# q, k and v computed row tile by row tile while the first modulation arrives by columns

## The reference

```
mod = c @ w_ada + b_ada                       # (1, 6*1024), c is (1, 1024)
sh1, sc1, gt1, sh2, sc2, gt2 = split(mod, 6)
h = rms_norm(x, g_pre_mix) * (1 + sc1) + sh1
proj = h @ w_in                               # 1024 x 5120
bg, cg, u, q, k, v, ga, gb = split(proj, [512]*6 + [1024]*2)
y_conv = short_conv(bg, cg, u) @ w_proj_conv
y_attn = stick_breaking_attention(q, k, v) @ w_proj_attn   # 8 heads of 64
merged = sigmoid(ga) * y_conv + sigmoid(gb) * y_attn
x = x + gt1 * rms_norm(merged @ w_out, g_post_mix)
...                                           # MLP with sh2, sc2, gt2; then layer two
```

## Time and profile before

| | |
|---|---|
| median of 3 runs | 845.17 us (841.72 to 845.89) |
| the profiled execution | 843.94 us, of which the span is 841.9 us |
| PE busy | 791.7 us, 94% of the span |
| DVE busy | 524.4 us, 62% |
| ACT busy | 379.3 us, 45% |
| POOL busy | 136.3 us, 16% |
| mean granted clock of PE | 0.946 |

### The profile page before, as it was taken

One profiled execution on the slowest core, in us unless ns is written; L12 is line 12 of the kernel. 1 busy time (PEld: TensorE's weight loads), 2 busy tenths in 40 slices (PEclk: granted clock), 3 DMA queues, 4 the chain that ended last, 5 costly groups with the idle time before them and its releaser, 6 DMA issues.

```text
span 841.9 us, 14038 instructions
## 1 busy us (share of the span) xinstructions
PE 791.7 (94%) x6051; PEld 754.8 (90%) x6051; DVE 524.4 (62%) x675; ACT 379.3 (45%) x520; POOL 136.3 (16%) x129
## 2 busy tenths in 40 slices
PE   3599999999979999999998999899799999999997
PEld 3599889999979999999997998587599999999997
DVE  5886677677336776644436799967654665555441
ACT  3443333443523545543434446577653543443441
POOL 1500110001000000000001399804000122221000
PEclk9599999999959999999997989999899999999998
DMA  9979565776603886565551441141614465654511
GB/s 350 359 261 307 183 201 191 238 272 200 200 1 106 254 277 209 191 210 166 191 157 51 150 152 50 50 151 51 199 51 151 151 220 181 200 175 151 188 39 51
DMA packets 123825, 146.00 MB, mean 173 GB/s; under 512 B 3988, under 2 KB 114804, under 8 KB 123764
## 3 DMA queue, kind: packets, MB, share of 16 engines
q1 hardware_dynamic: 122400, 143.32, 51.8%
q10 hardware_dynamic: 1364, 1.79, 0.7%
HBM read 144.05 MB, written 1.05 MB: 172 GB/s over the span
## 4 chain that ended last, share of the span: by engine, by line
PE 82%; DVE 10%; issue 4%; ACT 2%; DMA 1%; POOL 0%; SPq 0%; ACTq 0%; DVEq 0%; POOLq 0%
PE bank L575 70%; DVE mod_acc L1410 2%; PE bank L621 2%; PE bank L602 2%; ACT w_hi L1028 1%; DMA raw<-in_w_ada 1%; DVE score L1772 1%; DVE w_lo L1418 1%; DVE neg_max L1777 1%; DVE wide L1711 1%; PE bank L812 1%; DVE score L1795 1%; PE bank L798 1%; PE bank L610 1%; PE bank L783 1%
## 5 line engine op out<-in xcount | busy, mean ns | idle before, releaser
L1418 DVE TENSOR_TENSOR w_lo<-raw,w_hi 128x2048 fp32r<-128x2048 f32 (+1 forms) x108 | 245.9, 2280 | 140.6 <-ACT w_hi L1028 140.4
L1028 ACT ACTIVATE w_hi<-raw 128x2048 fp32r<-128x2048 f32 (+1 forms) x110 | 206.5, 1882 | 246.7 <-PE bank L575 227.5
L575 PE MATMUL bank<-act_hi,w_hi 128*128 128x256 f32 x816 | 237.2, 291 | 5.5 <-ACT act_hi L1184 2.7
L575 PE MATMUL bank<-act_lo,w_hi 128*128 128x256 f32 x816 | 234.8, 288 | 0.8 <-DVE act_lo L1678 0.4
L575 PE MATMUL bank<-act_hi,w_lo 128*128 128x256 f32 x816 | 234.1, 287 | 0.7 <-DVE w_lo L1418 0.7
L575 PEld LDWEIGHTS bank<-act_hi,w_hi 128*128 128x128 f32 x816 | 160.1, 196 | 9.1 <-issue 8.1
L575 PEld LDWEIGHTS bank<-act_lo,w_hi 128*128 128x128 f32 x816 | 160.0, 196 | 1.9 <-DVE act_lo L1678 0.7
L575 PEld LDWEIGHTS bank<-act_hi,w_lo 128*128 128x128 f32 x816 | 160.0, 196 | 0.9 <-DVE w_lo L1418 0.9
L575 PE MATMUL bank<-hidden_hi,w_hi 128*128 128x256 f32 x432 | 122.5, 284 | 0.8 <-DVE wide L1976 0.8
L575 PE MATMUL bank<-hidden_hi,w_lo 128*128 128x256 f32 x432 | 122.2, 283 | 0.0
L575 PE MATMUL bank<-hidden_lo,w_hi 128*128 128x256 f32 x432 | 122.2, 283 | 0.0
(11 more groups left out here) (268 smaller groups left out, 1052.3 us busy)
## 6 DMA issues: line engine op xcount, KB each, us to landing
raw<-in_w_in SPq DMA_DIRECT2D x31, 1024.0 KB, 5.8
raw<-in_w_ada SPq DMA_DIRECT2D x24, 1024.0 KB, 6.8
raw<-in_w_gate_up SPq DMA_DIRECT2D x22, 1024.0 KB, 5.1
raw<-in_w_mlp_in SPq DMA_DIRECT2D x16, 1024.0 KB, 5.7
raw<-in_w_mlp_out SPq DMA_DIRECT2D x16, 1024.0 KB, 5.2
raw<-in_w_out SPq DMA_DIRECT2D x8, 1024.0 KB, 7.1
raw<-in_w_down SPq DMA_DIRECT2D x8, 1024.0 KB, 5.1
raw<-in_w_down SPq DMA_DIRECT2D x4, 768.0 KB, 4.4
```

Source lines behind the costliest of these rows:

```text
L575: i = e.matmul(dst, lhs, rhs, start=start and k == 0 and m == 0 and n == 0, stop=stop and k == kt - 1 and n == 2, skip_group_check=True)
L1028: e.activation(w_hi[slot][:, 0:kt * n_cols], raw[i % N_RAW][:, 0:kt * n_cols], ACT.Copy).then_inc(hi_split, 1)
L1418: e.tensor_tensor(w_lo[slot][:, 0:kt * n_cols], raw[i % N_RAW][:, 0:kt * n_cols], w_hi[slot][:, 0:kt * n_cols].bitcast(F32), ALU.subtract) ...
```

## The change

The eight chunks of w_ada for shift and scale are replaced by eight transfers `ada1`, each of 128 columns of the shift and the same 128 of the scale over all 1024 rows (two transfers of 0.5 MB with pieces of 512 bytes). The six products of q, k and v are replaced by eight row-tile products: a chunk is one row tile (128 rows) by all 1536 columns (768 KB with pieces of 6 KB), and gives 36 matmuls (6 banks, 2 halves, 3 passes) that accumulate in six banks at once. The two kinds alternate in `plan`. For row tile k:

- DVE forms six of the eight terms of c times w_ada for both vectors at once (`first_rows`, 128x256 each), PE adds the other two straight from `raw` and sums over partitions (`first_modulation`, 6 matmuls of one column), DVE writes shift and scale of this tile (two operations on one column).
- DVE multiplies x_T by rstd (this was POOL's work), ACT applies scale and shift twice, once into act_hi and once in place, DVE subtracts for act_lo.
- The sums over partitions for tile k+1 stand in PE's program after half of the matmuls of tile k.

The sum of squares of x is taken by ACT over the rows as they landed, and spread to all partitions by two matmuls; the small row loads of the ACT queue go to SP's behind the first four chunks. q, k and v are evacuated by six copies on DVE after the last row tile, and `low` of the first chunk of c stands behind these copies in DVE's program. The remaining 14 products go through four banks, and 12 chunks of w_ada stand among the 18 products from c0 to the projections, two after every three. (Some semaphores are merged with others and their counts renumbered.)

```diff
-        ada_order = [(v, r) for v in (SCALE1, SHIFT1, GATE1, SHIFT2, SCALE2, GATE2) for r in range(ADA_CHUNKS)]
-        IN1, PC = 0, 20
+        ada_order = [(v, r) for v in (GATE1, SHIFT2, SCALE2, GATE2) for r in range(ADA_CHUNKS)]
+        IN1 = DT
+        PC = IN1 + len(in1_order)
...
-            if n % 2 and (n < 6 * ADA_CHUNKS or MLP1 + 2 <= n < MLP1 + 2 + 2 * ADA_CHUNKS):
+            if IN1 <= n < OUT1 and (n - IN1) % 3 != 2 or MLP1 + 2 <= n < MLP1 + 2 + 2 * ADA_CHUNKS and n % 2:
                 plan_ada()
-        for _ in range(2 * ADA_CHUNKS):
-            plan_ada()
+        def plan_first_ada(k):
+            plan.append(("ada1", k, [w("w_ada")[:, v * D + k * P:v * D + (k + 1) * P] for v in (SHIFT1, SCALE1)]))
+        for k in range(DT):
+            plan_first_ada(k)
+            plan_product(first_in1[k * P:(k + 1) * P, :])
...
+        FIRST_BANKS = {("q", 0): 4, ("q", 1): 5, ("k", 0): 6, ("k", 1): 0, ("v", 0): 1, ("v", 1): 2}
+        MOD1_BANKS = (7, 3)
...
-            for i in range(DT // 2):
-                sum_tiles((2 * i, 2 * i + 1), i == 0, i == DT // 2 - 1, (squared, i + 1))
-            modulation_sum(SCALE1)
-            transpose_rows(1)
-            transpose_rows(2)
-            modulation_sum(SHIFT1)
+            pe.wait_ge(x_rstd, 1)
+            for tt in range(TT):
+                t = e.matmul(b[:, tt * P:(tt + 1) * P], x_col[:, 1, tt:tt + 1].to_broadcast([P, P]), ident[:],
+                             start=tt == 0, stop=tt == TT - 1, skip_group_check=True)
+            t.then_inc(x_spread, 1)
+            def first_modulation(k):
...
+                pe.wait_ge(*landed(i))
+                for v in range(2):
+                    for r in range(DVE_ROWS, DT):
+                        e.matmul(b[:, v:v + 1], src[:, v, r, :], cols("c", r, 1), start=v == 0 and r == DVE_ROWS, stop=False,
+                                 skip_group_check=True)
+                pe.wait_ge(ada1_scaled, DVE_ROWS * (k + 1))
+                for v in range(2):
+                    t = e.matmul(b[:, v:v + 1], ada1_acc[:, k % 2, v, :], ones[:, 0:1], start=False, stop=True,
+                                 skip_group_check=True)
+                t.then_inc(mod1_summed, 1)
+            first_modulation(0)
+            for k in range(DT):
+                for c, (name, i) in enumerate(FIRST_BANKS):
+                    if c == 3 and k < DT - 1:
+                        first_modulation(k + 1)
...
+                    for m in range(2):
+                        for n, (wp, ap) in enumerate(((w_hi[slot], act_hi), (w_hi[slot], act_lo), (w_lo[slot], act_hi))):
...
+                t.then_inc(product_done, 1)
...
+            for k in range(DT):
+                high(k)
+                act.wait_ge(y_normed, k + 1)
+                act.wait_ge(mod1_set, 2 * k + 2)
+                e.activation(act_hi[:, k, :], y, ACT.Identity, scale=scale1[:, k:k + 1],
+                             bias=shift1[:, k:k + 1]).then_inc(tiles_hi, 1)
+                e.activation(y, y, ACT.Identity, scale=scale1[:, k:k + 1], bias=shift1[:, k:k + 1]).then_inc(tile_made, 1)
...
             for k in range(DT):
-                dve.wait_ge(tiles_hi, k + 1)
-                e.scalar_tensor_tensor(out=act_lo[:, k, :], in0=wide[1][:, k, :],
...
+                first_rows(k)
+                if k == 0:
+                    dve.wait_ge(x_rms, 1)
+                    e.reciprocal(x_col[:, 1, :], x_col[:, 0, :]).then_inc(x_rstd, 1)
+                first_norm(k)
+                first_modulation(k)
+                low(k)
+                dve.wait_ge(tile_made, k + 1)
+                e.tensor_tensor(act_lo[:, k, :], wide[1][:, k, :], act_hi[:, k, :].bitcast(F32),
+                                ALU.subtract).then_inc(tiles_lo, 1)
...
+            for name in ("q", "k", "v"):
+                for i in range(2):
+                    src = pair(bank[FIRST_BANKS[name, i]])
+                    dve.wait_ge(product_done, IN1)
...
+            stream_to(product_at[IN1])
+            low_after(product_at[IN1 - 2])
```

More of the change, by code:

```diff
@@ L347, in raw_view, with landed @@
             source = plan[i][2]
+            if plan[i][0] == "ada1":
+                return raw[i % N_RAW][:, 0:2 * DT * P].rearrange("p (v r c) -> p v r c", r=DT, v=2)
             kt, n_cols = source.shape[0] // P, source.shape[1]
             return raw[i % N_RAW][:, 0:kt * n_cols].rearrange("p (k c) -> p k c", k=kt)
+        def landed(i):
+            slot = i % N_RAW
+            return raw_landed[slot], sum(32 if plan[j][0] == "ada1" else 16 for j in range(slot, i + 1, N_RAW))
         rows_landed = [sem(f"rows{i}_landed") for i in range(3)]
@@ L521, in build, with ada1_at @@
         S_BANKS, T_BANK, O_BANK = (4, 5), 6, 7
-        mod_no = {v: n for n, v in enumerate((SCALE1, SHIFT1, GATE1, SHIFT2, SCALE2, GATE2))}
+        mod_no = {v: n for n, v in enumerate((GATE1, SHIFT2, SCALE2, GATE2))}
+        def ada1_at(k):
+            return plan.index(next(x for x in plan if x[0] == "ada1" and x[1] == k))
         def sync_program(e):
@@ L681, in stick_output @@
                          stop=True, skip_group_check=True).then_inc(stick_out, 1)
-            for p, (name, i) in enumerate(in1_order):
-                step = p - 6
-                if 0 <= step < HEADS:
+            for step in range(len(in1_order)):
+                p = IN1 + step
+                if step < HEADS:
                     stick_scores(step)
@@ L823, in compress @@
                     pe.wait_ge(cmp_paired_act, KV if not second else 2 * KV)
-                    pe.wait_ge(rms_set, 3 if second else 2)
-                pe.wait_ge(raw_landed[i % N_RAW], 16 * (i // N_RAW + 1))
+                    pe.wait_ge(rms_set, 2 if second else 1)
+                pe.wait_ge(*landed(i))
                 src = raw_view(i)
@@ L1060, in scalar_program @@
-            root(0, D, 1)
-            act.wait_ge(gains_set, 2)
-            act.wait_ge(x_copied, DT // 2)
+                e.activation(x_T[:, 2 * i:2 * i + 2, :], pair(bank[banks.bank["x", i]]), ACT.Copy).then_inc(x_copied, 1)
+            act.wait_ge(x_spread, 1)
+            e.activation(rstd[:], bank[banks.bank["x_rstd"]][:, 0:T], ACT.Copy).then_inc(rstd_set, 1)
             for k in range(DT):
-                e.activation(wide[1][:, k, :], x_T[:, k, :], ACT.Copy, scale=scale1[:, k:k + 1]).then_inc(y_scaled, 1)
@@ new lines, in first_rows @@
+            def first_rows(k):
+                i = ada1_at(k)
+                acc, src = ada1_acc[:, k % 2], raw_view(i)
+                dve.wait_ge(*landed(i))
+                if k >= 2:
+                    dve.wait_ge(mod1_summed, k - 1)
+                for r in range(DVE_ROWS):
+                    if r == 0:
+                        t = e.tensor_scalar(acc, src[:, :, r, :], cols("c", 0, 1), None, ALU.mult)
+                    else:
+                        dve.wait_ge(ada1_scaled, DVE_ROWS * k + r)
+                        t = e.scalar_tensor_tensor(out=acc, in0=src[:, :, r, :], scalar=cols("c", r, 1), in1=acc, op0=ALU.mult,
+                                                   op1=ALU.add)
+                    t.then_inc(ada1_scaled, 1)
```

304 lines of the change are left out of this document (178 added, 126 removed).

## The result

The changed kernel takes 849.14 us (median of 19 runs, 847.17 to 853.92) against 845.17 (841.72 to 849.24, 19 runs beside them). The ratio is 1.0055 with an interval of 1.0040 to 1.0071: half a per cent slower, where 848.5 was predicted. A later set of runs of the same kernel gave 848.43 and 1.0035 [1.0014, 1.0056].

A forecast was written before the change was run, and what follows sets the result against it. The chain of waits was read as DVE's multiplications of w_ada up to 33 us, then PE for long stretches from 37.84. Terms 1.3 + 2.3 + 0.4 gave +4.0 us on the profiled 843.94; 848.5 was predicted for the median, range 840 to 858.

The forecast's parts named there:

- The start: Head of the kernel: row tile 0 starts at 20.1, 17.7 us before the old 37.84.
- Tiles 0 and 1: First two row tiles: run at half clock at first, so act_lo of tile 2 comes at 36.7.
- I take 31 us: First row tiles: PE's full clock returns at 31 us, PE being dense from 26.2.
- the first rival: Head: full clock kept, or brought back by tile 0; c0 dense at 72.0, 840 to 843 us; chance 0.22.
- The clock in the tiles: Row tiles: 1.00 from about 31 to 72; rival of falls, 10.3 instead of 6.1 us each, 860, chance 0.12.
- The pace: Row tiles at full clock: 6.1 us each, set by DVE, with PE at 5.6.
- The transfers: Row tiles: 5.5 us a pair; rival of dear 512-byte pieces, 8.0 a pair, +11, 858, chance 0.08.
- The seam: Between tile 7 and c0: six copies 3.75 us, then `low` 2.2, PE idle; c0 dense at 77.7.
- The clock after the seam: Start of c0: 4.6 us at half clock, a loss of 2.3 us.
- The sum for the gate: Between c1 and u0: this sum moves behind b1, at 0 us.
- DVE as the bound behind c0: Rival, behind c0: w_ada work on DVE loses its cover, +4 to +7 us, 852 to 855; chance 0.10.
- the clock holds from the start: Rival, head: PE stays at full clock or tile 0 restores it; 840 to 843 us, chance 0.22.

The follow-up runs named there:

- `low` first with five rows: Changed kernel with `low` of c0 ahead of the six copies and five w_ada terms per tile on DVE instead of six: 845.73 us, ratio 1.0031.
- seven rows: Changed kernel with seven of the eight w_ada terms per tile on DVE instead of six, PE summing the other: 848.78 us, ratio 1.0064.
- act_order: Changed kernel with head 0's sigmoids ahead of u0's `high` in ACT's program: 844.72 us, ratio 0.9991.
- the seam closed: Changed kernel: q, k copied bank by bank, `low` of c0 before v's copies, sigmoids first on ACT, head 0's scans earlier on DVE: 844.42 us, ratio 1.0009.
- `low` of c0 first: Changed kernel with `low` of c0 ahead of the six copies in DVE's program: 840.67 us (0.9956), in another set 842.58 us (0.9984).

## Why the prediction was right, and where not

The time was right, 849.14 against 848.5, but by luck in good part. At the run of 240 the forecast was +4.0. In the execution that the forecast started from it is +2.2; on average of two profiles of each kernel it is +4.0. And that sum is made of two errors of 5 to 6 us in opposite directions: tiles that came sooner than forecast, and a wait that the forecast didn't have. The forecast's own sum, put on the median, is 849.2; no reason is given for 848.5. Small slips in the working (3.6 less 2.56 is 1.1, not 0.9; 18 matmuls of 0.213 from 20.1 on end at 23.9, not 23.6) change nothing here.

- *The start:* 18.06, not 20.1. In this execution the clock of 1.00 from the transposes of x fell only in 14 to 16 us. The spreading took 0.71 and not 1.19, the sums of tile 0 1.71 and not 2.65, and the first chunk was there at 10.04, not 10.6. In the second execution the spreading took 1.23, as forecast, and tile 0 started at 18.93.
- *Tiles 0 and 1:* the step that failed most is "I take 31 us" for the clock's return. It was back by 22, after PE had run dense since 18.06. act_lo of tile 2 came at 31.50 instead of 36.7. That is the head of the first rival, in its form "tile 0 brings it back", and its c0 at 72.0 is what was measured (72.1). The time of the return is not the kernel's alone: in ten of the eleven traces of the changed kernel and its versions act_lo of tile 1 came 6.9 to 7.9 us after that of tile 0, in the eleventh, of `low` first with five rows, 9.7, and the return was at 32.4, later than my 31.
- *The clock in the tiles:* 1.00 from 22 to 66. "TensorE: Matmul & The Clock Gate", section "HAM oscillation", of the Trainium skill warns of a fall in each tile where a loop waits for its data. With PE busy 41.14 of 42 us this trace hardly tests it; with seven rows PE was busy 25.97 of 30 us, waited in every tile, and the clock stayed at 1.00 there too.
- *The pace:* 6.03 for 6.1. The loop that I added up, DVE's program with PE's last sums, is 5.98 by the run with seven rows. What bounds the tiles by 0.05 us more is the ring through PE's first half tile, which I had not added up; I had compared the two loads, 6.1 and 5.6.
- *The transfers:* the pieces of 512 bytes held nothing up: 0.5 MB landed in 5.6 us (median of 16), and DVE did not wait for them in the tiles. But they were close behind. The 16 engines were busy 0.99 of the time with 312 GB/s, where pieces of 4 KB gave 410 at 1.03; by this share the pair of transfers for a tile takes about 6.0 us (0.99 of 6.03, an estimate) and not 5.5, so much faster tiles would probably have waited for them. "DMA: Bandwidth & Descriptors", section "Specifications", of the Trainium skill says that 512 B is enough for full rate. The share and the GB/s here do not bear that out, though no run moved such pieces alone.
- *The seam:* right. DVE waited 4.50 us for tile 7, then copies to 69.87 and `low` 2.21; from 66.17 to 72.1 is 5.9, forecast 6.1.
- *The clock after the seam:* right for c0 (0.51 in 72 to 76); with the transposes behind it half clock cost 1.9 us, forecast 2.3. Not in the sum is what followed. I named `low` as the work queued behind the copies on DVE, but did not follow it to the buffer that it frees, the transfer that waits for this buffer (5.15 us) and ACT's order behind that transfer. It took PE 3.66 us, and 2.05 more through c1 at half clock: 5.7, as much as c0 had come sooner than forecast (72.1 for 77.7).
- *The sum for the gate:* its move was put at 0, the row transposes at +0.4; the two stretches that they touch give -2.2 and +1.1.
- *DVE as the bound behind c0:* did not come. From u0 on a step lasts 8.06 us as before.

The rival "the clock holds from the start" predicted the head up to c0, but its 840 to 843 did not come, because of the wait of head 0. act_order shows the mechanism: with that wait gone the time is 844.72, level with the kernel before.

What stays open: what the versions lose behind the run of 240, where the seam closed starts it at 144.54 and has a median of 844.42, and how much of each median is the clock's luck. Executions of one kernel differ by 4 to 12 us here, and that is more than the steps between the better versions. The best, `low` of c0 first, measured 0.9956 and 0.9984.

## What to carry to other kernels

When an instruction moves back in an engine's program, follow three things behind it: what it frees, which transfer starts when it is free, and which work stands in order behind the arrival of that transfer on another engine. Put work whose input is ready ahead of a wait for a transfer. Where two engines hand a tile back and forth, add up every loop of waits that closes on itself, through both engines, and not the two loads: the longest loop is the pace. Where two loops are equal, shifting work in either direction makes it slower. And look at two executions of each kernel before you trust a difference of a few microseconds to its cause.

## What the runs showed of the hardware

POOL's multiplication of beta and the remainders (`weight`, two instructions) has no fixed price. Five of the changed kernel's first eight take 1.00 to 1.07 us, one 1.47, and two that DVE's long additions for `mod_acc` run beside take 2.87 and 1.99. POOL's timeline and below it DVE's, of the changed kernel:

```profile
81.14 2.87 POOL L2160 TENSOR_TENSOR weight<-beta,remain 128x128 f32<-128x128 f32 x2 [77.50 <-DVE remain L1674]
89.42 1.99 POOL L2160 TENSOR_TENSOR weight<-beta,remain 128x128 f32<-128x128 f32 x2 [5.41 <-DVE remain L1674]
98.45 1.01 POOL L2160 TENSOR_TENSOR weight<-beta,remain 128x128 f32<-128x128 f32 x2 [7.03 <-issue]
```

```profile
80.90 2.61 DVE L1514 SCALAR_TENSOR_TENSOR mod_acc<-raw,col_tile,mod_acc 128x1024 f32<-128x1024 f32 x2
...
89.65 2.85 DVE L1514 SCALAR_TENSOR_TENSOR mod_acc<-raw,col_tile,mod_acc 128x1024 f32<-128x1024 f32 x2
```

In the first case each of POOL's two instructions outlasts one of DVE's two, and POOL ends 0.5 us after DVE's pair. In the kernel before, head 0's took 1.00 at 82.10, with DVE idle. With the seam closed DVE had one such addition there instead of two (70.24, 1.31 us); head 0's took 2.34 at 69.71 and again ended 0.5 us after it.

The Trainium skill has the rule in "SBUF — State Buffer", section "Who interferes with whom": a DVE instruction with two inputs in SBUF and a GpSimd instruction that reads SBUF share a port, and the later one waits for the whole of the other. These additions have two inputs in SBUF, and the trace agrees by its overlaps; no run here took all of DVE's additions away. In the changed kernel the two meet in the very chain that holds up c1, where, by the 1.00 without them, it is 1.9 us of the 3.66 that PE waits.

The clock's return has no fixed time either. In the kernel before PE was busy all of 38 to 44 in both executions; the window 42 to 44 has 0.50 in one and 1.00 in the other. In the changed kernel it was back by 22 us, within 4 us of dense work, and with `low` first and five rows at 32.4, after 13 us.

The column PEclk can miss a fall. In the second execution of the changed kernel it reads 1.00 from 14 us on, but its chain has the prices of half clock:

```profile
12.86 1.23 PE bank L698 x4
...
18.93 3.99 PE bank L746 x17
```

The same instructions take 0.71 and, from tile 1 on, 2.30 at full clock. Five of the eleven traces show this at their start, so the durations of the matmuls decide.
